# Scaling attention probabilities per key tile for four heads at once on GpSimd, in a hybrid GLA and NSA layer

## What is computed

```python
s = jnp.einsum('bqhgd,bihd->bhgqi', qblk, kc)                 # compressed: 63 keys
p_cmp = jax.nn.softmax(jnp.where(valid, s, -1e30), axis=-1) * valid
o_cmp = jnp.einsum('bhgqi,bihd->bqhgd', p_cmp, vc)
...
_, sel = lax.top_k(imp, n_sel)        # n_sel = min(16, 1024 // 64): all blocks
s = jnp.einsum('bqhgd,bhqnld->bhgqnl', qblk, k_g)             # selected
p_slc = jax.nn.softmax(where(m, s, -1e30))
o_slc = jnp.einsum('bhgqnl,bhqnld->bqhgd', p_slc, v_g)
...
s = jnp.einsum('bqhgd,bkhd->bhgqk', qblk, kw)                 # window of 512
p_win = jax.nn.softmax(jnp.where(mw, s, -1e30), axis=-1)
o_win = jnp.einsum('bhgqk,bkhd->bqhgd', p_win, vw)
...
o = g[..., 0:1] * o_cmp + g[..., 1:2] * o_slc + g[..., 2:3] * o_win
```

## Time and profile before

| | |
|---|---|
| median of 3 runs | 819.66 us (819.59 to 821.3) |
| span of the profiled execution | 817.9 us |
| PE busy in it | 800.5 us, 98% |
| DVE, ACT, POOL busy | 516.0, 436.7, 427.1 us |
| in the attention stretch, 400 to 602 us | DVE 193.3, ACT 191.8, POOL 174.0 of 202 us |

### The profile page before, as it was taken

How to read it: one execution, slowest core, us unless ns; L and a number is a source line. 1 busy time by engine, 2 the same in 40 slices (tenths; PEclk the granted TensorE clock), 3 DMA queues, 4 the chain that set the end, 5 groups by cost and what they waited for, 6 DMA issues and landing times.

```text
span 817.9 us, 12432 instructions
## 1 busy us (share of the span) xinstructions
PE 800.5 (98%) x4578; PEld 680.4 (83%) x4578; DVE 516.0 (63%) x1008; ACT 436.7 (53%) x910; POOL 427.1 (52%) x371
## 2 busy tenths in 40 slices
PE   7999999999999999999999999999999999999995
PEld 7878888888988888888888889889878888887884
DVE  3782459951861804576999999999970263435426
ACT  4601154222233014758999999999972534426424
POOL 3302126355041121567779989899735464553554
PEclk9999999999999999999999999999999999999998
DMA  9511111201111111263200000000048332222237
GB/s 297 128 53 45 33 49 39 53 26 52 28 50 41 26 44 35 77 159 72 65 1 1 2 1 1 1 1 1 2 169 319 85 97 90 91 91 77 91 119 240
DMA packets 39918, 58.36 MB, mean 71 GB/s; under 512 B 11281, under 2 KB 17713, under 8 KB 39858
## 3 DMA queue, kind: packets, MB, share of 16 engines
q1 hardware_dynamic: 39570, 56.52, 23.3%
q0 software_dynamic: 288, 1.05, 0.8%
HBM read 49.16 MB, written 5.25 MB: 67 GB/s over the span
## 4 chain that ended last, share of the span: by engine, by line
PE 84%; DVE 11%; ACT 2%; issue 1%; POOL 1%; DMA 0%; DVEq 0%; SPq 0%; ACTq 0%; POOLq 0%
PE psum L1060 45%; PE psum L1353 6%; PE psum L1331 3%; PE psum L1332 3%; PE psum L1175 3%; PE psum L1376 3%; PE psum L1377 3%; DVE gla_att L2189 2%; DVE pT_lo L2363 2%; DVE gla_b L2180 1%; DVE p_slc L2335 1%; PE psum L982 1%; PE psum L981 1%; PE psum L980 1%; PE psum L1086 1%
## 5 line engine op out<-in xcount | busy, mean ns | idle before, releaser
L1850 POOL TENSOR_TENSOR w_lo<-w_raw,w_hi 128x512 fp32r<-128x512 f32 x124 | 180.1, 1457 | 306.2 <-ACT w_hi L1499 305.7
L1499 ACT ACTIVATE w_hi<-w_raw 128x512 fp32r<-128x512 f32 x124 | 78.2, 634 | 307.5 <-PE psum L1060 294.1
L1060 PE MATMUL psum<-w_hi,xT_hi 128*128 128x512 f32 x256 | 100.8, 394 | 0.6 <-DVE gla_state_b L2239 0.6
L1060 PE MATMUL psum<-w_hi,xT_lo 128*128 128x512 f32 x256 | 99.7, 389 | 0.0
L1060 PE MATMUL psum<-w_lo,xT_hi 128*128 128x512 f32 x256 | 99.6, 389 | 0.0
L2363 DVE TENSOR_TENSOR pT_lo<-psum,pT_hi 128x512 fp32r<-128x512 f32 (+1 forms) x148 | 95.1, 656 | 6.0 <-ACT pT_hi L1719 3.0
L1910 POOL TENSOR_SCALAR p_slc<-p_slc,gate_over_sum 128x512 f32<-128x512 f32 (+7 forms) x60 | 95.5, 1606 | 1.3
L1719 ACT ACTIVATE pT_hi<-psum 128x512 fp32r<-128x512 f32 (+1 forms) x148 | 82.3, 572 | 8.6 <-PE psum L1353 6.7
L1331 PE MATMUL psum<-kT,qT_hi_lo 128*128 128x384 f32 (+3 forms) x192 | 66.8, 350 | 0.9 <-DVE neg_max L2335 0.7
L1332 PE MATMUL psum<-kT,qT_hi_lo 128*128 128x384 f32 (+3 forms) x192 | 60.6, 328 | 0.0
L1376 PE MATMUL psum<-pT_hi,v_hi_lo 128*128 128x512 f32 x132 | 59.5, 451 | 0.6 <-DVE pT_lo L2363 0.6
(11 more groups left out here) (305 smaller groups left out, 1964.4 us busy)
## 6 DMA issues: line engine op xcount, KB each, us to landing
w_raw<-in_w_in SPq DMA_DIRECT2D x56, 256.0 KB, 2.7
w_raw<-in_ple_gate SPq DMA_DIRECT2D x32, 256.0 KB, 2.5
w_raw<-in_w_out SPq DMA_DIRECT2D x30, 256.0 KB, 2.6
x_tok<-in_x SPq DMA_DIRECT2D x8, 512.0 KB, 6.4
h_tok<-in_x SPq DMA_DIRECT2D x8, 512.0 KB, 6.1
kT<-kT SPq DMA_DIRECT2D x12, 256.0 KB, 3.6
out<-h_tok SPq DMA_DIRECT2D x6, 512.0 KB, 5.5
w_raw<-in_ple_proj SPq DMA_DIRECT2D x8, 256.0 KB, 2.5
```

Source lines behind the costliest of these rows:

```text
L1060: mm = pe.matmul(out, lhs, rhs, start=(first and n == 0), stop=(final and n == 2))
L1499: act.activation(w_hi(i)[:, 0:w], w_in(i)[:, 0:w], ACT.Copy).then_inc(s_whi, 1)
L1850: pool.tensor_tensor(w_lo(i)[:, 0:w], w_in(i)[:, 0:w], w_hi(i)[:, 0:w].bitcast(F32), ALU.subtract).then_inc(s_wlo, 1)
```

## The change

Scaling of the two long branches is done per unit: one instruction multiplies the 128 keys of one tile for all four heads (128 x 4 x 128) with `RG` broadcast along the keys, as a tensor_tensor. It is on GpSimd for all steps but the last, whose four units go to VectorE. ScalarE scales nothing any more. `turn` of every unit waits for its own unit's scaling instead of the first unit's waiting for the whole step. The table of `attention_timeline` has the new operations (700 ns on VectorE, 1290 ns on GpSimd), and the search orders everything anew, with the same number of rounds and the same seed.

```diff
-    scaler = ("C", "APPP", "PPAP")
...
-    def scalers(s):
-
-        return "VAVA" if s == len(steps) - 1 else scaler[steps[s][2]]
...
+    def unit_scaler(u):
+
+        s, i = units[u]
+        if steps[s][2] == 0:
+            return "C"
+        return "V" if s == len(steps) - 1 else "P"
...
-                e = scalers(s)[g]
-                ops["scale" + e, n] = e if e != "P" else "G", {"V": 0.7, "A": 0.84, "P": 2.5}[e] * nk + {"V": 210, "A": 285, "P": 285}[e], s
-                after["scale" + e, n] = [("gates", s)]
...
+            e = unit_scaler(u)
+            if not few:
+                ops["scale" + e, u] = ("V", 700, s) if e == "V" else ("G", 1290, s)
+                after["scale" + e, u] = [("gates", s)]
             ops["turn", u] = "P", 380 if few else 600, s
-            after["turn", u] = ([("scale" + scalers(s)[g], GRP * s + g) for g in range(GRP)]
-                                if steps[s][2] else [("cscale", s)]) + [("low", u - TRING), ("stack_lo", soon - 1)]
+            after["turn", u] = [("cscale", s) if few else ("scale" + e, u), ("low", u - TRING), ("stack_lo", soon - 1)]
...
-            if i == 0:
-                for e in sorted(set(scalers(s))):
-                    pe.wait_ge(scaled[e], scaled_count(e, s))
+            pe.wait_ge(scaled[unit_scaler(u)], scaled_count(u))
...
-        def scale_act(n):
...
-            act.activation(x, x, ACT.Copy, scale=RG[:, n:n + 1]).then_inc(s_norma, 1)
...
-        def scale_pool(n):
-            s, g = divmod(n, GRP)
-            nk = span(*steps[s][1:])[1]
+        def scale_pool(u):
+            s, i = units[u]
+            x = probs(s)[:, :, i * P:(i + 1) * P]
             pool.wait_ge(s_rg, s + 1)
-            pool.tensor_scalar(probs(s)[:, g, 0:nk], probs(s)[:, g, 0:nk], RG[:, n:n + 1], None,
+            pool.tensor_tensor(x, x, RG[:, GRP * s:GRP * s + GRP].unsqueeze(2).to_broadcast([P, GRP, P]),
                                ALU.mult).then_inc(s_norm, 1)
...
-        def scale_dve(n):
...
-            dve.tensor_scalar(x, x, RG[:, n:n + 1], None, ALU.mult).then_inc(s_normd, 1)
+            dve.tensor_tensor(x, x, RG[:, GRP * s:GRP * s + GRP].unsqueeze(2).to_broadcast([P, GRP, P]),
+                              ALU.mult).then_inc(s_normd, 1)
```

More of the change, by code:

```diff
@@ L365, in build_program @@
     s_normd = sem("probs_scaled_dve")
-    s_norma = sem("probs_scaled_act")
     s_pt = sem("probs_turned")
@@ L560, in scores_at, with scaled_count @@
         return PSUM[:, b:b + 2].rearrange("p a b -> p (a b)")[:, first:first + nk], 512 - first
-    def scalers(s):
-        return "VAVA" if s == len(steps) - 1 else scaler[steps[s][2]]
-    def scaled_count(e, s):
-        return sum(scalers(t).count(e) for t in range(s + 1))
+    def unit_scaler(u):
[3 more added lines that the diff above has]
+        return "V" if s == len(steps) - 1 else "P"
+    def scaled_count(u):
+        return sum(1 for v in range(u + 1) if unit_scaler(v) == unit_scaler(u))
     stacks = [("k", 0, 0), ("k", 1, 0)] + [("q", h, 0) for h in range(4)] + [("c", 0, 0)] \
@@ L736, in attention_timeline @@
             after["wo_mm", n] = [("wo_lo", n), ("values", last), ("z_lo", 7)]
-        kinds = ["z_turn", "z_hi", "z_lo", "wo_load", "wo_hi", "wo_lo", "wo_mm", "gla_rms", "gla_gate", "values", "half", "output", "gated", "low", "high", "turn", "gate", "gates", "cmax", "cexp", "csub", "cmask", "cscale", "scaleV", "scaleA", "scaleP",
+        kinds = ["z_turn", "z_hi", "z_lo", "wo_load", "wo_hi", "wo_lo", "wo_mm", "gla_rms", "gla_gate", "values", "half", "output", "gated", "low", "high", "turn", "gate", "gates", "cmax", "cexp", "csub", "cmask", "cscale", "scaleV", "scaleP",
                  "exponent", "csum", "mask_max", "cscore", "score", "gate_z", "gate_mul", "first_mul", "gate_sig", "stack_lo", "stack_hi", "stack_turn",
@@ L805, in build_program @@
     timeline = attention_timeline()
-    scaled = {"C": s_normc, "V": s_normd, "A": s_norma, "P": s_norm}
+    scaled = {"C": s_normc, "V": s_normd, "P": s_norm}
     def probs(s):
@@ L1725, in output_half @@
             act.activation(OB[:], bank(6 + j % ORING)[64:128], ACT.Copy).then_inc(s_ob, 1)
-        def scale_act(n):
-            s, g = divmod(n, GRP)
-            nk = span(*steps[s][1:])[1]
-            act.wait_ge(s_rg, s + 1)
-            x = probs(s)[:, g, 0:nk]
-            act.activation(x, x, ACT.Copy, scale=RG[:, n:n + 1]).then_inc(s_norma, 1)
         def z_hi(u):
@@ L1746, in _ @@
                 compressed_exponent(n)
-            elif kind == "scaleA":
-                scale_act(n)
             elif kind == "high":
@@ L2348, in gate_over_sum, with scale_dve @@
             dve.reciprocal(RG[:, n], SU[:, n]).then_inc(s_rcp, 1)
-        def scale_dve(n):
-            s, g = divmod(n, GRP)
-            nk = span(*steps[s][1:])[1]
+        def scale_dve(u):
+            s, i = units[u]
+            x = probs(s)[:, :, i * P:(i + 1) * P]
             dve.wait_ge(s_rg, s + 1)
-            x = probs(s)[:, g, 0:nk]
-            dve.tensor_scalar(x, x, RG[:, n:n + 1], None, ALU.mult).then_inc(s_normd, 1)
+            dve.tensor_tensor(x, x, RG[:, GRP * s:GRP * s + GRP].unsqueeze(2).to_broadcast([P, GRP, P]),
+                              ALU.mult).then_inc(s_normd, 1)
         def tile_lo(u):
```

## The result

The changed kernel takes 823.96 us (median of 5 runs, 823.48 to 825.2) against 821.1 (5 runs): ratio 1.0042, 95% interval 1.003 to 1.0054. It is slower by some 3.4 us, outside the predicted range. Later comparisons go by the kernel before on the chips of the experiments, 819.58 to 820.63 (9 to 26 runs each). The profiled execution is the changed kernel's longest run (span 823.3, time 825.2) and that of before one of the shortest, so the two traces overstate the loss: 5.4 us between spans.

What follows compares the result with a forecast made beforehand. VectorE was taken to bound attention, with ScalarE making it miss its turn. Terms: 3.6 + 2.7 + 0.4 us off, 1.8 + 1.4 on, -3.5 us from 819.66, giving 816.2 us; range 811.5 to 822.5.

Steps and rivals of the forecast that it cites:

- "3.6 us off in full": Attention, 400 to 602 us: VectorE's waits on ScalarE vanish once ScalarE stops scaling, 3.6 us off.
- the 58 ns of the earlier trace: Attention's value matmul pairs: first takes 452 ns, second 394; over 127 pairs read as 7.4 us of PE's late starts.
- The rival "nothing happens: PE is the bound already": Attention: PE already bounds, so relieving the others leaves the time unchanged; chance 0.21 together with the dear GpSimd instruction.
- "I take them off as well": Attention: turns waiting per tile let PE begin steps sooner, removing VectorE's waits for PE, 2.7 us off.
- GpSimd's price: Attention: the new scaling form takes 1047 ns per tile on GpSimd, 134.0 us for 128, none on the path.
- The last step, +1.8: Attention's last step: four tensor_tensor replace two tensor_scalar on VectorE, fully counted, +1.8 us.
- Collisions, +1.4 for two hits: Attention: VectorE and GpSimd collide on SBUF in two of eight VectorE instructions (late gate_mul, new scalings), +1.4 us.
- 380 to 400 us, 0.4 off: Just before the attention stretch: VectorE has 3.7 us idle there, of which 0.4 us is counted off.
- All behind attention the same length: After attention: PE is full from 622 to 800 us, so that work only starts sooner, at unchanged length.
- The rival "slower": Attention: all eight SBUF collisions hit, or a late order; +3.2 us, 822.9 us, chance 0.21.
- 5.0 us of recovery: Attention, in the slower rival: 3.6 + 2.7 / 2 us of waits surely recovered even when VectorE is held up.
- fifth hit: Attention, slower rival: from five SBUF collisions on, costs of 5.7 us exceed the 5.0 recovered.

Runs made afterwards that it cites:

- e1: The kernel before, in its own order, with ScalarE's scaling of a head cut to one key; 820.77 us, ratio 1.000.
- f1: The kernel before with low halves made for 256 of 512 columns and the second value matmul reading pT_hi, relieving VectorE; 817.37 us, ratio 0.9961.
- h1: The kernel before, in its order, with per-tile scaling on GpSimd in all steps but the last, which stays scaled by heads; 821.92 us, ratio 1.0016.
- e2: The kernel before, in its order, with per-tile scaling in all steps, the last step's four tiles on VectorE; 822.39 us, ratio 1.0028.
- e3: The changed kernel in its order, with the last step's four tiles scaled on GpSimd instead of VectorE; 822.11 us, ratio 1.0021.
- e4: The changed kernel in its order, with VectorE's four last-step scalings cut to one key per head; 821.82 us, ratio 1.0024.
- d1: The kernel before with the p_tok and h_tok loads behind attention issued four w_raw pieces later; 819.71 us, ratio 0.9993.
- d2: The changed kernel with the p_tok and h_tok loads behind attention issued four w_raw pieces later; 822.76 us, ratio 1.0037.
- c3: The changed kernel with last step by heads, GpSimd tile priced 1050, p_tok and h_tok loads later, seed 5, late gate_mul on GpSimd; 816.92 us, ratio 0.9964.

## Why the prediction was wrong

**"3.6 us off in full" for ScalarE: 0.** Measured alone by e1. The waits of VectorE on ScalarE were read as time to be won, but in the middle it is mostly TensorE's rate that sets the pace (20 us less for VectorE there bring 1.7 us, f1; TensorE's relief 3.7, f2), and a wait of VectorE for ScalarE there is slack. The error began a step earlier: 202 us were read as one stage with VectorE "the fullest member", and PE's 2.5 us of idleness and the 58 ns of the earlier trace rows were spread over it as late starts. In truth 1.67 of the 2.5 us idle lie in the first 30 us, and the 58 ns are no lateness. The rival "nothing happens: PE is the bound already" described well what became of the middle, where the loss is 6.3 us after 6.0, and was given too little.

**"I take them off as well", 2.7 us for turns per tile: 0.** VectorE's listed waits on PE for scores fall from 2.7 us to 1.6 (0.8 + 0.5 + 0.3), and with them nothing else: the middle loses 6.3 us as it lost 6.0. h1 has the form there and the order of before, and loses 6.1.

**GpSimd's price: right.** 1043 and 1044 ns against 1047; busy 130.3 against the 134.0 forecast for 128 tiles, the whole relief unused. PE's turns waited for it twice, 0.7 us in all, which the forecast had named as a sign of being wrong; it is too little to be the loss.

**The last step, +1.8: too much.** 1.0 us in the order of before, with no scaling hit (e2 less h1), and 1.5 to 1.7 in the new one (e3, e4), there with the two collisions in it.

**Collisions, +1.4 for two hits: right in number, not in worth.** None of the four late gate_mul was hit, so the 0.3 us of before went; two of the four scalings were, by 0.69 and 0.48 us, 1.2 us of VectorE's time. What they cost the kernel is already in the 1.5 to 1.7 us of the last step. In h1 the gate_mul was hit instead.

**380 to 400 us, 0.4 off: wrong.** There the new order loses 1.5 us more (360 to 400) and gets 0.8 back by 430. The forecast had called a move of over a microsecond ahead of 400 us a sign of being wrong. The other orders lost from 2.3 to 4.0 us at 360 to 400, so this is a matter of the draw.

**All behind attention the same length: nearly.** 622:800 is matched by 628:806, 177.27 against 177.28, but the first 15 us behind attention hold the late weights, 1.25 us in this trace. As far as d1 and d2 tell (0.6 and 0.4 us, within their intervals), the kernel before loses as much there on average, so this is a difference between two traces and not shown to be one between the kernels.

So the sum fails in its two gains, 3.6 and 2.7 us, for which the runs show nothing. Leave them and the 0.4 out, and the rest, 1.8 + 1.4 = +3.2 us, looks like the measured 3.4 (0.42% of 820). That is luck: the last step with its collisions explains 1.5 to 1.7 us. The other 1.7 to 1.9 us are spread over the core and the order. h1, the form in the core alone, costs 1.3 us, and the traces of after show 0.7 net ahead of 430 and 0.3 in the middle; how the rest divides is open. The rival "slower" had named the last step and the collisions with their price, but let 5.0 us of recovery stand against them; without it no fifth hit was needed.

## What to carry to other kernels

Before a wait is booked as a gain, cut the stage until each piece has one bound, and ask in each what the bounding engine would do with the time; relief of another engine is worth little there (ScalarE's nothing here, VectorE's 1.7 us of 20). In a balanced ring test each engine by relieving it alone and both together: here 3.2, 3.7 and 10.0 us. Costs at the ends of a stage, where the pipeline is short of work, count (1.0 to 1.7 us here), while relief of an engine that is not the bound of its middle does not. Here the freed engine paid only when it took work off the full one at a place where that one is the bound, as in c3.
